# Five matmuls per weight tile in place of six: tokens split 280/240, high and low parts of the right side in one moving operand

## Reference

```python
def half_ffn(x, g, w_gate, w_up, w_down):
    h = rmsnorm(x, g)
    return 0.5 * ((jax.nn.silu(h @ w_gate) * (h @ w_up)) @ w_down)
```

## Time and profile before

| what | value |
|---|---|
| median of 3 runs | 2365.05 us (2364.11 to 2367.05) |
| profiled execution, span from the first to the last instruction | 2362.3 us |
| mean granted PE clock | 0.980 |
| PE, PEld busy | 2245.2, 2157.4 us |
| DVE, ACT, POOL busy | 1117.2, 789.2, 104.3 us |
| matmul instructions on PE | 17745 |

### The profile page before, as it was taken

One profiled execution on the slowest core, in us unless ns is written; L12 is line 12 of the kernel. 1 busy time (PEld: TensorE's weight loads), 2 busy tenths in 40 slices (PEclk: granted clock), 3 DMA queues, 4 the chain that ended last, 5 costly groups with the idle time before them and its releaser, 6 DMA issues.

```text
span 2362.3 us, 43636 instructions
## 1 busy us (share of the span) xinstructions
PE 2245.2 (95%) x17745; PEld 2157.4 (91%) x17745; DVE 1117.2 (47%) x1672; ACT 789.2 (33%) x1072; POOL 104.3 (4%) x178
## 2 busy tenths in 40 slices
PE   6999999998889899999999999999998799999997
PEld 5999999998778799999999999999995479999996
DVE  3444433674346564444333444433667744444332
ACT  4222222343223453222223222222456533222222
POOL 0000000100012200000000000000003200000000
PEclk9999999998989999999999999999998999999998
DMA  3333233432110133333333333333323123333331
GB/s 104 98 96 89 87 91 90 118 82 63 45 24 1 25 106 90 89 92 94 90 89 91 96 89 89 92 91 89 90 81 109 45 90 90 91 95 89 92 89 52
DMA packets 351440, 195.71 MB, mean 83 GB/s; under 512 B 9902, under 2 KB 345930, under 8 KB 351336
## 3 DMA queue, kind: packets, MB, share of 16 engines
q1 hardware_dynamic: 344368, 172.09, 25.4%
q0 software_dynamic: 6064, 19.86, 2.8%
q10 hardware_dynamic: 912, 2.42, 0.3%
HBM read 186.43 MB, written 8.04 MB: 82 GB/s over the span
## 4 chain that ended last, share of the span: by engine, by line
PE 65%; DVE 4%; ACT 3%; issue 1%; POOL 0%; DMA 0%; POOLq 0%; ACTq 0%; DVEq 0%
PE PS L1701 57%; PE PS L1808 5%; PE PS L2146 1%; PE PS L2114 0%; PE PS L1987 0%; DVE skX L1573 0%; DVE Dm L1406 0%; DVE skX L1588 0%; PE PS L2098 0%; PE PS L2135 0%; ACT skX L991 0%; ACT skL L999 0%; ACT skL L1000 0%; ACT skL L997 0%; ACT skY L994 0%
## 5 line engine op out<-in xcount | busy, mean ns | idle before, releaser
L1701 PE MATMUL PS<-hh,whi 128*128 128x260 f32 x3600 | 732.1, 285 | 5.5 <-ACT xT L1050 4.2
L1701 PE MATMUL PS<-hh,wlo 128*128 128x260 f32 x3600 | 728.3, 284 | 0.0
L1701 PE MATMUL PS<-hl,whi 128*128 128x260 f32 x3600 | 727.5, 284 | 0.0
L1092 DVE TENSOR_TENSOR wlo<-stage,whi 128x1024 fp32r<-128x1024 f32 x337 | 412.3, 1224 | 461.6 <-ACT whi L663 450.7
L1701 PEld LDWEIGHTS PS<-hh,whi 128*128 128x128 f32 x3600 | 559.7, 190 | 7.7 <-ACT xT L1050 4.3
L1701 PEld LDWEIGHTS PS<-hh,wlo 128*128 128x128 f32 x3600 | 558.0, 189 | 0.0
L1701 PEld LDWEIGHTS PS<-hl,whi 128*128 128x128 f32 x3600 | 557.1, 189 | 0.0
L663 ACT ACTIVATE whi<-stage 128x1024 fp32r<-128x1024 f32 x337 | 352.8, 1048 | 259.6 <-PE PS L1701 245.7
L1701 PE MATMUL PS<-act_h,whi 128*128 128x260 f32 x1408 | 284.0, 283 | 0.0
L1701 PE MATMUL PS<-act_h,wlo 128*128 128x260 f32 x1408 | 283.1, 282 | 0.0
L1701 PE MATMUL PS<-act_l,whi 128*128 128x260 f32 x1408 | 282.5, 282 | 0.0
(11 more groups left out here) (376 smaller groups left out, 1770.6 us busy)
## 6 DMA issues: line engine op xcount, KB each, us to landing
stage<-in_ffn_w_gate SPq DMA_DIRECT2D x88, 512.0 KB, 3.8
stage<-in_ffn_w_up SPq DMA_DIRECT2D x88, 512.0 KB, 3.8
stage<-in_ffn_w_down SPq DMA_DIRECT2D x64, 512.0 KB, 3.9
stage<-in_w_in_e SPq DMA_DIRECT2D x28, 512.0 KB, 3.8
stage<-in_ffn_w_down SPq DMA_DIRECT2D x32, 384.0 KB, 3.4
stage<-in_w_in_o SPq DMA_DIRECT2D x20, 512.0 KB, 3.8
stage<-in_w_out_e SPq DMA_DIRECT2D x8, 512.0 KB, 4.1
stage<-in_w_out_o SPq DMA_DIRECT2D x8, 512.0 KB, 4.0
```

Of the source, the lines that this page charges most:

```text
L1092: dve.tensor_tensor(wlo[:, slot, :], stage[:, s % STAGE_SLOTS, :], whi[:, slot, :].bitcast(F32), ALU.subtract).then_inc(lo_ready, 1)
L1701: mm = pe.matmul(psum[:, half, :], w, x(k)[:, half * HALF:(half + 1) * HALF], start=start and k == 0 and w is hi and x is rhs_hi, stop=sto ...
```

## The change

RIGHT is 240 and LEFT 280. High and low parts of the activations lie side by side in one buffer (`hx` [k][2][TOK], `act_x`; `hh`, `hl`, `act_h`, `act_l` are views of it). Per tile PE issues five matmuls: left high, then one of 480 columns with the right high and right low columns into two halves of bank 2n+1, left low, and with `wlo` the right high and left high columns. So the two sums hi·hi and hi·lo of the right side lie apart in PSUM (`right(n, 0)` and `right(n, 1)`) and someone has to add them. In `take()` ACT first copies the low one to a new buffer `rlow` (`low_part`, which waits for the unit's end and stands right behind `split_ahead` in ACT's order), DVE adds the high one and then scales; in `update()` DVE adds both to `xT`, one after the other.

```diff
+    RIGHT = TOK * 6 // 13
+    LEFT = TOK - RIGHT
+    LT, RT = slice(0, LEFT), slice(LEFT, TOK)
...
+        def left(n, rows=P):
+            return PS[0:rows, 2 * n, 0:LEFT]
+        def right(n, low, rows=P):
+            return PS[0:rows, 2 * n + 1, low * RIGHT:(low + 1) * RIGHT]
...
-        hh = sb("hh", [P, KD, TOK], F32R, shared)
-        hl = sb("hl", [P, KD, TOK], F32R, shared)
+        hx = sb("hx", [P, KD, 2, TOK], F32R, shared)
+        hh, hl = hx[:, :, 0, :], hx[:, :, 1, :]
...
+            def low_part(b, taken, per, t, q, n, rows=P):
+                act.wait_ge(unit_done, b + per * t + q + 1)
+                if not isinstance(t, int) or taken + per * t + q:
+                    act.wait_ge(low_added, taken + per * t + q)
+                act.activation(rlow[0:rows, :], right(n, 1, rows), ACT.Copy).then_inc(low_out, 1)
...
                 for n in range(QKV, E_TILES):
                     split_ahead(b + 1, 4, 0, n)
+                    low_part(b + 1, taken + 1, 4, 0, n, tile_pair(n))
                     if n == GATES_AT:
                         gdn_gates()
...
-            def take(dst, psum, scale=1.0):
-                return dve.scalar_tensor_tensor(out=dst, in0=psum, scalar=scale, in1=two(rstd[:]), op0=ALU.mult,
-                                                op1=ALU.mult)
+            def take(dst, n, number, scale=1.0, rows=P):
+                dve.scalar_tensor_tensor(out=dst[:, LT], in0=left(n, rows), scalar=scale, in1=rstd[0:rows, LT],
+                                         op0=ALU.mult, op1=ALU.mult)
+                dve.wait_ge(low_out, number + 1)
+                dve.tensor_tensor(dst[:, RT], right(n, 0, rows), rlow[0:rows, :], ALU.add).then_inc(low_added, 1)
+                dve.wait_ge(low_added, number + 1)
+                return dve.scalar_tensor_tensor(out=dst[:, RT], in0=dst[:, RT], scalar=scale, in1=rstd[0:rows, RT],
+                                                op0=ALU.mult, op1=ALU.mult)
...
+            def update(s, m, done, n, scale):
+                xl, xr = (xT[:, bass.ds(m, 1), t].rearrange("p a b -> p (a b)") for t in (LT, RT))
                 dve.wait_ge(unit_done, done)
-                dve.scalar_tensor_tensor(out=x, in0=psum, scalar=scale, in1=x, op0=ALU.mult, op1=ALU.add)\
+                dve.scalar_tensor_tensor(out=xr, in0=right(n, 0), scalar=scale, in1=xr, op0=ALU.mult, op1=ALU.add)\
+                   .then_inc(x_part, 1)
+                dve.scalar_tensor_tensor(out=xl, in0=left(n), scalar=scale, in1=xl, op0=ALU.mult, op1=ALU.add)
+                dve.wait_ge(x_part, KD * s + m + 1)
+                dve.scalar_tensor_tensor(out=xr, in0=right(n, 1), scalar=scale, in1=xr, op0=ALU.mult, op1=ALU.add)\
                    .then_inc(x_ready, 1)
...
-                    for w, x in ((hi, rhs_hi), (hi, rhs_lo), (lo, rhs_hi)):
-                        for half in range(2):
-                            last = w is lo and k == tiles - 1
-                            mm = pe.matmul(psum[:, half, :], w, x(k)[:, half * HALF:(half + 1) * HALF],
-                                           start=start and k == 0 and w is hi and x is rhs_hi, stop=stop and last)
+                    x, high = rhs(k)
+                    both = PS[:, 2 * n + 1, 0:2 * RIGHT].rearrange("p (a b) -> p a b", a=2)
+                    first, last = start and k == 0, stop and k == tiles - 1
+                    pe.matmul(left(n), hi, x[:, high, LT], start=first, stop=False)
+                    pe.matmul(both, hi, x[:, 0:2, RT], start=first, stop=False)
+                    pe.matmul(left(n), hi, x[:, 1 - high, LT], start=False, stop=False)
+                    pe.matmul(right(n, high), lo, x[:, high, RT], start=False, stop=last)
+                    mm = pe.matmul(left(n), lo, x[:, high, LT], start=False, stop=last)
```

More of the change, by code:

```diff
@@ L81, in build_step @@
     TAIL = CW - 1 + TS
+    assert RIGHT % 2 == 0 and 2 * RIGHT <= 512 and LEFT <= 512
     assert TOK % 4 == 0 and DM % P == 0 and FF % P == 0 and TP % P == 0 and KF % 2 == 0 and KD % 4 == 0
@@ L91, in build_step @@
     FIRST, UNITS = {}, 0
+    TAKEN, takes = {}, 0
     for stage_name, f in STAGES:
@@ L95, in build_step @@
             UNITS += n
+            if name in ("in", "mix_e", "mix_o"):
+                TAKEN[name + str(f)] = takes
+                takes += n
     LAST_NORM = len(STAGES)
@@ L1145, in body @@
                             dve.wait_ge(prod_ready, n - 1)
-                        take(two(tmp[:, a, :]), pair(2 * a)).then_inc(gate_read, 1)
+                        take(tmp[:, a, :], 2 * a, TAKEN[f"in{f}"] + 4 * t + 2 * a).then_inc(gate_read, 1)
                         split_ahead(b, 4, t, 2 * a + 1)
@@ L1150, in body @@
                             dve.wait_ge(act_lo, n - 1)
-                        take(two(tmp[:, 2 + a, :]), pair(2 * a + 1)).then_inc(up_read, 1)
+                        take(tmp[:, 2 + a, :], 2 * a + 1, TAKEN[f"in{f}"] + 4 * t + 2 * a + 1).then_inc(up_read, 1)
                         dve.wait_ge(up_read, n + 1)
@@ L1199, in body @@
                         split_ahead(b, 4, t, a)
-                        update(s, 4 * t + a, b + 4 * t + a + 1, pair((a + 2) % 4), 1.0)
+                        update(s, 4 * t + a, b + 4 * t + a + 1, (a + 2) % 4, 1.0)
                         add_square(s + 1, 4 * t + a, a % 2)
@@ L1229, in project_e @@
                 dve.wait_ge(rstd_ready, s + 1)
-                dve.scalar_tensor_tensor(out=two(small[:]), in0=pair(2)[0:96], scalar=1.0, in1=two(rstd[0:96, :]),
-                                         op0=ALU.mult, op1=ALU.mult).then_inc(pe_read, 1)
+                take(small[:], 2, TAKEN["mix_e0"], rows=96).then_inc(pe_read, 1)
                 def body(t):
@@ L1242, in body @@
                             dve.wait_ge(silu_e, n - 1)
-                        take(two(rawE[:, q % 2, CW - 1:CW - 1 + TOK]), pair(q)).then_inc(pe_read, 1)
+                        take(rawE[:, q % 2, CW - 1:CW - 1 + TOK], q, TAKEN["mix_e0"] + 1 + n).then_inc(pe_read, 1)
                         conv(n, q % 2, rawE, histG, lambda k, n: PRM["gdn_conv_w"] + k * QKV + n, tailE,
@@ L1251, in project_e @@
                     dve.wait_ge(unit_done, b + 2 + n)
-                    take(two(prE[:, n, :]), pair(tile_pair(n)), DKA ** -0.5 if n < AK else 1.0).then_inc(pe_read, 1)
+                    take(prE[:, n, :], tile_pair(n), TAKEN["mix_e0"] + 1 + n, DKA ** -0.5 if n < AK else 1.0).then_inc(pe_read, 1)
                     if n == GATES_AT:
@@ L1504, in project_o @@
                     if n >= KR:
-                        take(two(prO[:, n, :]), pair(n % 4 if n < 2 * KR else n % 2),
+                        take(prO[:, n, :], n % 4 if n < 2 * KR else n % 2, TAKEN["mix_o0"] + n,
                              HDC ** -0.5 if OQ <= n < OK else 1.0).then_inc(po_read, 1)
@@ L1510, in project_o @@
                             dve.wait_ge(xo_ready, n - 1)
-                        take(two(rawO[:, n % 2, CW - 1:CW - 1 + TOK]), pair(n % 4)).then_inc(po_read, 1)
+                        take(rawO[:, n % 2, CW - 1:CW - 1 + TOK], n % 4, TAKEN["mix_o0"] + n).then_inc(po_read, 1)
                         conv(n, n % 2, rawO, histR, lambda k, n: PRM["rg_conv_w"] + k * KR + n, tailO,
@@ L1688, in _, with unit @@
         def _(pe):
-            def unit(s, number, rhs_hi, rhs_lo, tiles, psum, start, stop, ready=None):
+            def unit(s, number, rhs, tiles, n, start, stop, ready=None):
                 slot = s % SPLIT_SLOTS
@@ L1774, in project, with out_proj @@
                 loop(pe, 1, tiles // 4, body)
-            def out_proj(s, name, parts, hi, lo):
+            def out_proj(s, name, parts, rhs):
                 b = FIRST[name]
@@ L1788, in project_e @@
                 b = FIRST["mix_e0"]
-                unit(b, b, h_hi_tile, h_lo_tile, KD, pair(2), True, True, lambda k: pe.wait_ge(h_lo, KD * s + k + 1))
+                unit(b, b, h_tile, KD, 2, True, True, lambda k: pe.wait_ge(h_lo, KD * s + k + 1))
                 project(s, b + 1, QKV, pe_read, 1)
@@ L1794, in project_e @@
                     pe.wait_ge(pe_read, n + 1 if n >= GLA_AT + 2 else n)
-                    unit(b + 1 + n, b + 1 + n, h_hi_tile, h_lo_tile, KD, pair(tile_pair(n)), True, True)
+                    unit(b + 1 + n, b + 1 + n, h_tile, KD, tile_pair(n), True, True)
                     if L2_AT <= n < L2_AT + HB:
```

73 lines of the change are left out of this document (40 added, 33 removed).

## The result

The changed kernel takes 2408.95 us (median of 4 runs, 2407.91 to 2410.23), the kernel before 2364.95 beside it: a ratio of 1.0183, 95% interval 1.0169 to 1.0197. It is slower by 44 us; the forecast was 13.8, and the range ended at 2398. The profiled execution has a span of 2407.9 us, 45.6 more than before.

The account below looks back on a forecast made before the run. PE's matmul stream was taken to bound the ffn stages, with PE waiting for DVE and ACT in the mix stages. From 2365.05 us, -19.8 for the stream and +33.5 of costs gave 2378.8; range 2308 to 2398.

Parts of the forecast that it names:

- The stream: All 2632 weight tiles, five matmuls in place of six: 7.5 ns less per tile, -19.8 us (bounds -8.7 and -31.1).
- Rival 2: PE's stream: all columns are slow, only 3.3 ns per tile or less come back, 2390 us; chance 0.25.
- Rival 1: PE's stream: weight loads set the 120.1 ns, the long matmul hides one; 36.9 ns less per tile, 2310 us; chance 0.18.
- Rival 4: Merged matmul: an operand of two pieces might not stream at one column per cycle, 2399 us; chance 0.05.
- (a): The 12 projections with a convolution: longer takes make DVE's round longer than PE's unit, +5 us (3.6 to 6.5).
- (b): Unit 12: ACT's gate chain starts later, behind the copy, and DVE's scans behind it: +5 us (0 to 5).
- (c): Units 15 to 17: the squares for the norm come behind the copy, after the unit's end, +4.5 us (3.5 to 5).
- (d): Units 20, 22, 24, 26: vtA, attT and POOL's select behind the low part, 8.8; longer takes, 2.7; +11.5 us (6 to 13).
- (e): mix_o: ACT's gate activations come behind the unit's low part and the last take is 0.54 longer, +3 us (0.5 to 6).
- (f): End of the kernel: the last update stands alone behind the end of the stream, +0.5 us.
- (g): PE's clock, 555 to 650 us: longer gaps add a third to the 12 us lost at half clock, +4 (0 to 12).
- Rival 3: Mix stages: waits are cheap, 20 us of costs paid, the stream gains the whole 31.1, 2354 us; chance 0.12.

Follow-up runs that it names:

- late_all: As late_gla, with the copy also behind the gate chains (units 12, 13), the squares (units 14 to 17) and mix_o's two sigmoids: 2369.93 us.
- late_gla: Changed kernel, but from unit 18 on ACT's copy of the low part goes behind those of vtA, attT, kdtA and prE: 2382.19 us.

## Why the prediction was wrong

- **The stream** (taken as 7.5 ns per tile, 19.8 us): 7.0 measured in the span between norms. The size is right by luck, for the reason given for it isn't. It was the middle between a price per matmul of 11.8 and one of 3.3; the runs show 0.7 to 3.2 ns per matmul, the rest with the columns, and the remainder of the 7 is that 280 and 480 columns happen to stream at 0.451 and 0.455 ns per column where 260 take 0.462. Rival 2 had the mechanism, but its gain of 3.3 was too small and its time, 2390, 19 us too short. Rival 1 (a spacing of 120 ns set by the load) fell: a matmul of 240 columns is followed after 109.6 ns, and 480 columns take 218.5, not 203.3. Rival 4 fell: 480 columns in two pieces or in one take the same.
- **(a) +5**: +6.6. The DVE round became longer than PE's unit (5.9 us to 8 x 0.714 = 5.7); the wait ahead of the gates grew by 5.65 us.
- **(b) +5**: +6.9, of which 6.57 - 1.43 = 5.1 is the wait itself. Right, to the engine and the row.
- **(c) +4.5**: +7.2. The three waits are 0.98, not 1.5 (2.9 in all); the wait on `prE` grew by 1.1; and some 3.4 are PE's work at the half clock, which came back in late_all with the waits.
- **(d) +11.5** for waits: 8.9 for the four, and five waits on `prE` and on what comes of it longer by 0.2 to 0.6 each, 11.4 us. Right.
- **(e) +3**: +3.9, but in the main not for the reason given: moving the copies at the gates changed nothing (late_all). A round of DVE between two of its waits for ACT has three takes, and it is 19.84 us (1791.58 to 1811.42) where it was 19.05 (1745.84 to 1764.89 in the kernel before), some 3.2 us over four rounds; no run took the takes alone.
- **(f) +0.5**: +1.6; what the other 1.1 are was not taken apart.
- **(g) +4 for the clock is the step that failed.** The late_gla run puts it at 18.7 us in the GLA stretch alone, and late_all adds 3.4 in (c). The forecast took a third more of the 12 us that the half level cost before, as if the gaps only got longer. But each of the four chunks got a new gap in its middle, where before PE had only one pair of gaps, ahead of the unit. In the stretch the half level went from about 25 to 68 us. It is there that most of the way from 13.8 to 44 lies. By the table, the rows of costs sum to +57.0 where the forecast had 33.5 less the 2.9 us that their own tiles gain, 26.4 more, of which 14.7 are the clock in the one stretch and 3.4 that in (c); the rows of the stream sum to -11.4 in place of -16.8, since besides the 7.0 ns per tile they hold a later start of the first unit and a longer wait ahead of the first QKV unit (1.81 us for 1.27), and some 3 us that no run took apart.
- **Rival 3** (the waits are cheap) fell with all of its parts.
- **The range.** The direction was right, with 0.58 on it; the range of 2308 to 2398 was 11 us short. Its upper bound counted the clock at 12 at most, and it took 42 for the costs without a working, where the upper bounds of the parts add up to 48; even with 48 it would have ended at 2404.

## What to carry to other kernels

Where an in-order engine gets a short new operation that waits for the end of a unit, ask what stands behind it in that engine's order, and put it behind all that doesn't depend on it: here 6 us of copies cost 41.5, and moving copies within the order gave 39 back. Price a new gap on PE as itself plus the work that then runs at half clock; in this kernel the second was twice the first. And an edit that gains in the stream and loses in the mixed stages should be made in the stream alone: that version takes 2353.7 us, where the change everywhere takes 2409 and the kernel before 2365.

## What the runs showed of the hardware that was not expected

- This stream of fp32r matmuls takes 0.451 to 0.462 ns per column at the full clock, not 0.417, for lengths from 220 to 512, in one piece of memory or two; at the half clock 480 columns take 400.0 ns, and nothing of the kind shows. What limits it is open, and so is why 280 columns (surplus 9.7) stream better than 264 (11.3) and 300 (13.2).
- A short matmul has a price that its neighbour pays: behind one of 220, 240 and 256 columns the next took 10.8, 6.1 and 0.3 ns longer than others of its length, and at the half clock 13.3 ns longer behind one of 240.
- Four gaps of 2.2 us, one in each chunk of 23 us that already had two gaps, took the clock of that stretch from 0.87 to 0.72, and taking them away brought back 0.85.
